# Gates, compressed scores and heads of the sparse mixer in one stage; last norm in two operations, written out in pieces

## What the kernel computes

```
proj = h @ w_in                       # 1024 columns of queries, 48 of gates
gate = sigmoid(proj[..., 1024:])      # 3 gates for each head
s = q @ k_cmp.T ; p_cmp = masked_softmax(s, cmp_end <= t)     # 15 compressed keys
p_slc = masked_softmax(q @ k_slc.T, ...)                      # causal
p_win = masked_softmax(q @ k_win.T, ...)                      # causal, window 512
out = gate0 * p_cmp @ v_cmp + gate1 * p_slc @ v_slc + gate2 * p_win @ v_win
y = out @ w_o
```

## Time and profile before

| | us |
|---|---|
| median of 3 runs | 3552.88 (3550.22 to 3556.15) |
| the profiled execution | 3553.42 |
| its span | 3551.7 |
| TensorE busy in the span | 3305.5 (93%) |
| VectorE, ScalarE, GpSimd busy | 2252.0, 1786.2, 1139.1 |
| mean granted clock of TensorE, as a share of 2.4 GHz | 0.961 |

### The profile page before, as it was taken

One profiled execution on the slowest core, in us unless ns is written; L12 is line 12 of the kernel. 1 busy time (PEld: TensorE's weight loads), 2 busy tenths in 40 slices (PEclk: granted clock), 3 DMA queues, 4 the chain that ended last, 5 costly groups with the idle time before them and its releaser, 6 DMA issues. The chain is left out here.

```text
span 3551.7 us, 64847 instructions
## 1 busy us (share of the span) xinstructions
PE 3305.5 (93%) x20998; PEld 2947.0 (83%) x20998; DVE 2252.0 (63%) x4498; ACT 1786.2 (50%) x3650; POOL 1139.1 (32%) x1179
## 2 busy tenths in 40 slices
PE   7997999999899998997999999978899889999997
PEld 7987898997599867996889999877579868899996
DVE  7966687878586553779445555554468784455555
ACT  6556545448444444557444444453345564444443
POOL 2233021226022004467633333200006676233332
PEclk9998999999999999999999999987599999999999
DMA  5540587882387443440555555633034315555554
GB/s 182 178 137 30 201 321 259 316 299 96 101 309 259 161 148 136 161 148 10 185 167 183 188 184 183 200 117 101 1 131 163 116 42 188 168 183 186 185 185 144
DMA packets 163126, 590.87 MB, mean 166 GB/s; under 512 B 18596, under 2 KB 19236, under 8 KB 162728
## 3 DMA queue, kind: packets, MB, share of 16 engines
q1 hardware_dynamic: 143824, 521.95, 44.5%
q10 hardware_dynamic: 19160, 67.18, 4.9%
HBM read 588.00 MB, written 1.06 MB: 166 GB/s over the span
## 5 line engine op out<-in xcount | busy, mean ns | idle before, releaser
L319 PEld LDWEIGHTS ps<-hT,parts 128*128 128x128 f32 x12864 | 1598.4, 194 | 82.6 <-DVE parts L143 38.1
L319 PE MATMUL ps<-hT,parts 128*128 128x256 f32 x12864 | 1615.4, 285 | 50.2 <-DVE parts L143 28.1
L143 DVE TENSOR_TENSOR parts<-ring,parts 128x512 fp32r<-128x512 f32 x1754 | 1167.3, 700 | 569.5 <-ACT parts L138 560.4
L138 ACT ACTIVATE parts<-ring 128x512 fp32r<-128x512 f32 x1930 | 1156.1, 628 | 575.7 <-PE ps L319 543.1
L319 PE MATMUL ps<-parts,gatedT 128*128 128x512 f32 x4128 | 1011.5, 397 | 7.6 <-DVE parts L143 7.6
L319 PEld LDWEIGHTS ps<-parts,gatedT 128*128 128x128 f32 x4128 | 765.3, 190 | 175.3 <-POOL gatedT L1055 7.9
L1191 POOL TENSOR_TENSOR gatedT<-acted,iota 128x256 fp32r<-128x256 f32 x264 | 167.2, 633 | 1411.6 <-PE ps L319 1196.7
L143 POOL TENSOR_TENSOR parts<-ring,parts 128x512 fp32r<-128x512 f32 x176 | 225.3, 1304 | 664.2 <-ACT parts L138 663.6
L1162 ACT ACTIVATE acted<-ps 128x256 f32<-128x256 f32 x264 | 101.9, 386 | 589.4 <-PE ps L319 589.4
L1194 POOL TENSOR_TENSOR gatedT<-acted,gatedT 128x256 fp32r<-128x256 f32 x264 | 313.4, 1187 | 20.6
L1175 DVE TENSOR_TENSOR acted<-acted,big 128x256 f32<-128x256 f32 x176 | 74.9, 425 | 362.2 <-ACT acted L1162 362.2
(11 more groups left out here) (342 smaller groups left out, 2185.1 us busy)
## 6 DMA issues: line engine op xcount, KB each, us to landing
ring<-wts SPq DMA_DIRECT2D x965, 512.0 KB, 3.5
big<-mod_wts ACTq DMA_DIRECT2D x112, 512.0 KB, 4.8
big<-rows SPq DMA_DIRECT2D x15, 512.0 KB, 5.3
big<-mod_bias ACTq DMA_DIRECT2D x14, 512.0 KB, 4.3
big<-mod_rows SPq DMA_DIRECT2D x4, 512.0 KB, 5.2
big<-peer_keys SPq DMA_DIRECT2D x2, 1024.0 KB, 5.5
x<-x_in SPq DMA_DIRECT2D x1, 1024.0 KB, 5.2
big<-s_bc ACTq DMA_DIRECT2D x4, 256.0 KB, 3.3
```

Of the source, the lines that this page charges most:

```text
L138: act.activation(self.part(n, half, 0), self.raw(n, half), ACT.Copy).then_inc(self.hi_done, 1)
L143: v.tensor_tensor(self.part(n, half, 1), self.raw(n, half), self.part(n, half, 0).bitcast(F32), ALU.subtract).then_inc(self.lo_done, 1)
L319: last = pe.matmul(out, a(x), b(y), start=start and x + y == 0, stop=stop and x == 1)
```

## The change

- `nsa` becomes one projection (now with `ahead=1`) and one stage for all the rest. In it TensorE first does the compressed scores of both query blocks, each matmul now against 128 columns (15 of them used, the rest overwritten or unread), then the gates, also 128 columns wide in place of 48, then the heads.
- The wide items come first: 32 items, wide 0 to 15, narrow 16 to 31, with no barrier between. Score banks in PSUM are four in place of two, the buffers `pr`, `prT` and `small` four in place of two, and score(i) waits for the exponentials of item i-4.
- The mask is added in place in PSUM and only to the last 128 keys of each branch (256 columns in all also for a wide item). Maximum and exponential read PSUM.
- The compressed weights are written to a padded tile `cs4`. Their copy `keep` stands on VectorE inside items 0 and 1.
- At the end of the stage ScalarE and GpSimd split the first tile of the output projection.
- `residual_ln` forms `(z - mean) * ln_g` and then `* 1/sqrt + ln_b`, one `scalar_tensor_tensor` each, all on VectorE; eps goes in as the bias of the square root, whose table is loaded up front; the output is sent as three DMAs from the same stage: 512 KB, 256 KB, 256 KB. The last stage goes.

```
-    with stage(k, "g_in b_in rooted eps_in centred gained dve") as (s, block):
+    with stage(k, "g_in b_in moments rooted finished out_done dve") as (s, block):
+        pieces = ((0, slice(0, D)), (1, slice(0, HALF)), (1, slice(HALF, D)))
+            for n, (tt, cols) in enumerate(pieces):
+                sp.wait_ge(s["finished"], n + 1)
+                sp.dma_start(rows[:, tt, cols], k.x[:, tt, cols]).then_inc(s["out_done"], 16)
...
+                st.done(v.scalar_tensor_tensor(k.tmp[:, tt, :], k.x[:, tt, :], aggr(tt)[:, 0:1], k.row[:, 0, :],
+                                               ALU.subtract, ALU.mult))
+                v.wait_ge(s["rooted"], tt + 1)
+                st.link(v.reciprocal(inverse(tt), root(tt)))
...
+                v.scalar_tensor_tensor(k.x[:, tt, cols], k.tmp[:, tt, cols], inverse(tt), k.row[:, 1, cols],
+                                       ALU.mult, ALU.add).then_inc(s["finished"], 1)
```

```
-                    [(mask, k.dram["mask"]), (cmask, k.dram["cmask"])], entry=SplitEntry(k, other_columns(k)))
+                    [(mask, k.dram["mask"]), (cmask, k.dram["cmask"])], entry=SplitEntry(k, other_columns(k)), ahead=1)
+    items = [(qt, h) for qt in (1, 0) for h in range(NH)]
...
+            def compressed(qt):
+                for h in range(NH):
+                    last = pe.matmul(k.ps[:, 4 * (1 - qt) + 2 + h % 2, 16 * h:16 * h + P], qT[rows(h), h // 2, queries(qt)],
+                                     keys_c[rows(h), NCMP * (h // NR):NCMP * (h // NR) + P], start=True, stop=True)
...
+            def score(i):
+                if i >= 4:
+                    pe.wait_ge(s["exped"], 2 * (i - 3))
...
+            compressed(1)
+            compressed(0)
             for half in range(2):
                 k.w.wait_split(pe, first, half)
...
-                        last = products(pe, k.ps[:, tt, 0:48], lambda lo: k.hT[:, lo, kc, tt * P:(tt + 1) * P],
-                                        lambda lo: k.w.part(first, half, lo)[:, q * P:q * P + 48], kc == 0, kc == KC - 1)
+                        last = products(pe, k.ps[:, tt, 0:P], lambda lo: k.hT[:, lo, kc, tt * P:(tt + 1) * P],
+                                        lambda lo: k.w.part(first, half, lo)[:, q * P:q * P + P], kc == 0, kc == KC - 1)
...
+            pe.wait_ge(s["c_maxed"], 1)
+            score(0)
+            score(1)
+            pe.wait_ge(s["c_maxed"], 2)
+            compressed_turn(0, 1)
+            compressed_turn(1, 0)
+            for i in range(n_items + 3):
+                if i + 2 < n_items:
+                    score(i + 2)
+                if 1 <= i <= n_items:
+                    turn(i - 1)
+                if i >= 3:
+                    values(i - 3)
...
+                    block_ = two(score_bank(i), qt)[:, :, nk - P:nk]
+                    v.wait_ge(s["scored"], i + 1)
+                    st.done(v.tensor_tensor(block_, block_, bc(mask[:, T - P:T].unsqueeze(1), [P, 2, P]), ALU.add))
...
+        @block.gpsimd
+        def _(pool):
+            k.w.split_lo(pool, first + 1)
```

## The result

The changed kernel takes 3513.74 us (median of four executions, 3506.64 to 3530.11), the kernel before 3554.31 beside it: ratio 0.9894, 95% interval 0.9858 to 0.9930. The forecast was 3530 in a range of 3508 to 3556. The profiled execution took 3514.44 against 3553.42: 39.0 less, where my sum had 23.3. (Medians here are over all executions of a kernel; the ratios are of means, and leave out the executions more than 1.5% above the fastest of their kernel.)

What follows compares the result with a forecast made beforehand. The prediction took TensorE at half clock in the mixer as the bound. Mixer -21.4, edge +1.8, and norm and output -3.7 sum to -23.3 from 3553.4, giving 3530 us, range 3508 to 3556.

Steps and rivals of the forecast that it cites:

- compressed scores: Mixer's first work: 64 matmuls priced from a head's narrow scores, nearly all at half clock, 18.0 us.
- gates: Mixer, after the compressed scores: 48 matmuls at half clock, 0.21 us each whatever the width, 10.1 us.
- edge to the output projection: Mixer's end: splits after the last copy delay the barrier 3.3 us, the next stage saves 1.5; net +1.8 us.
- norm and output: Kernel's end: VectorE chain done at 3543.8, last 256 KB landing 3.3 us after issue; -3.7 us.
- its own last sign: Closing test: mixer about 128 us; forecast wrong if the clock differs, all else together being worth 10 us.
- The fill: Mixer, between gates and steady heads: VectorE's path puts first transposes 8.1 us after the gates, third after 14.7.
- The same 14.9 us: Heads: full clock returns after 14.9 us of unbroken wide items, as in the kernel before, losing 7.4 us.
- The narrow items: Heads' second part: VectorE becomes the bound at 2.05 us an item against TensorE's 1.7, at full clock.
- the first rival in its second form: Mixer: clock stays up or returns within some 4 us, then the fill loses it again: 3518; whole rival's chance 0.24.
- The rival of the other side: Heads: the new order breaks the unbroken wide stretch, so the clock never lifts: +55, 3585; chance 0.08.
- That narrow items fall back to half clock: Rival, heads: VectorE's gaps put narrow items at 3.43 us in place of 2.05: +22, 3552; chance 0.13.
- In-place work in PSUM slow enough to matter: Part of a rival, heads not shortened: 0.3 us more on each VectorE step, +15, 3545; whole rival's chance 0.07.

Runs made afterwards that it cites:

- E5: The changed kernel itself, measured again unaltered: median 3507.41 us, five executions between 3497 and 3557.
- E1: The changed kernel with dummy matmuls on TensorE where it stood still while the heads fill: 3496.81 us, ratio 0.9846.
- E6: The kernel before, unmerged, with 128 columns for compressed and gate matmuls and dummy matmuls where TensorE stands still: 3531.26 us, ratio 0.9933.
- E7: The changed kernel with each block's compressed scores ordered by row half, eight heads then the other eight, not alternating: 3524.82 us, one execution.
- E10: The changed kernel with fill dummies, early output-projection split, no root table behind the query projection, and four dummies at each edge: 3490.63 us, ratio 0.9831.
- E4: The changed mixer with the last norm and output stage as in the kernel before: 3527.2 us, ratio 0.9961.
- E3: The changed kernel with the narrow items ahead of the wide ones, as before the change: 3543.68 us, ratio 0.9974.
- E2: The changed kernel with compressed matmuls put back to 15 columns and gate matmuls to 48: 3522.05 us, ratio 0.9909.

## Why the prediction was right in its range and off in its steps

| step | forecast | measured (profiled executions) |
|---|---|---|
| start of the stage | 2447.5 | 2447.3 |
| compressed scores | 18.0 | 5.4 |
| gates | 10.1 | 5.5 |
| from the gates to the third item's transposes | 14.7 | 13.7 |
| from there to the last matmul | 82.6 | 86.3 |
| mixer against before | -21.4 | -35.9 |
| edge to the output projection | +1.8 | +1.05 |
| norm and output | -3.7 | -4.9 |
| elsewhere | 0 | +0.8 |
| sum | -23.3 | -39.0 |

By its own last sign ("It is wrong if the clock differs from this") the prediction's course of the clock was wrong, and the mixer took 113.6 us where that sign had about 128. The number came into the range because the range was wide and because a part of the error was taken back: 17.2 us too much for scores and gates, 3.7 too little for the heads. That is in part luck; the same kernel measured again (E5) has its median at 3507.4, just below the range.

- **The reading of the bound was right**: TensorE at half clock was the matter, and the place. E1 shows it by adding nothing but matmuls that nobody reads, E6 by adding such matmuls and widening two kinds of matmul with the stages left as they were.
- **Compressed scores, the largest miss (12.6 us).** Two errors. I took the scores of a head as the nearest row; the compressed ones alternate between the two halves of the array's rows, which in E7 is worth 0.07 of 0.17 us each at half clock (E10 has them at 3.84 / 64 = 0.06 each at full clock, not 0.15). And I let half clock last through them, because the heads' narrow work had never lifted it. It was back 3.4 us later. The row of the old 15-column matmuls, which alternate in the same way, was in the trace (shown at E7) and would have told the price: 3.60 / 32 = 0.11 each at half clock.
- **Gates.** That 128 columns cost what 48 did was right: at half clock 0.20 us per instruction before and 9.59 / 48 = 0.20 in E6. The step failed by the clock alone, for they ran at full: 5.58 / 48 = 0.12.
- **The fill.** 1.0 us less than forecast. The terms listed up to the first head's transposes add up to 7.7, not 8.1; measured were 7.6.
- **The clock in the heads.** "The same 14.9 us" was wrong in size and in kind: 41 us in the profiled execution, 24 in E5, 58 in E4. One observation does not give a duration; what settles the time of the return is not known. From the third item's transposes to the last matmul the changed kernel takes 86.3 us, and E1, at full clock throughout, 2541.58 - 2469.63 = 71.95. So the half clock cost 14.3 us there, where I had 7.4; the same stretch at full clock was 3.2 us shorter than my 75.2. Together that is the +3.7 of the table.
- **The narrow items.** VectorE was not the bound; 1.94 us each, TensorE without gaps. My 0.3 of waits in its loop was too much. That they would hold the full clock was right.
- **The rivals.** The measured course is the first rival in its second form, a clock back within 4 us that the fill loses again; I had put it at 3518 with the family at 0.24, and the time is 3513.7. The likeliest case, one long half-clock stretch, did not come. The rival of the other side, a clock that never lifts in the heads, is not disproved: E5 had 3557 once, with a mean clock of 0.958, and E3, E2 and E4 have such executions, at 3552 to 3565, with 0.954 to 0.960 (in E3's trace the clock lifts only at the very end of the heads). Its price of 3585 was too high, mostly because it stood on scores and gates at half clock. That narrow items fall back to half clock did not come in the changed kernel, but they stay there when the fill has dropped it first (E3). In-place work in PSUM slow enough to matter did not show: the narrow items follow each other in 1.94 us.
- **The edge.** +1.05, not +1.8: the next stage starts 3.67 us after the last copy (2558.48 to 2562.15), before 1.21 (2594.63 to 2595.83). That is 2.5 us more, where I had 3.3. Of it 1.4 us come back up to the first matmul, as reckoned (1.5).
- **The norm.** The chain on VectorE took the forecast 13.7 us (3495.99 to 3509.01 + 0.66). The gain is 1.2 us more than forecast, since 256 KB landed in 2.1 us, not 3.3; I had taken the row of the same size, and it was a load into the core, not a write of the output.

## What to carry to other kernels

Where TensorE is busy without a break and yet slow, read its granted clock first, then look at what it did just before the fall: here TensorE was busy 2.34 of 4.1 us, with two pauses of 1.0 and 0.75 us, and fell to half clock; the busy share of the whole span (94%) does not show it. That cost 17 us, and twenty matmuls into an unused bank gave them back and took most of the scatter away with them. Look in the traces for the work in which the clock came back and put that first (here the alternating scores of 128 columns). Put work in which it never came back, here the narrow items, behind it. Before a duration is taken over from a similar row, compare which rows of the array follow each other, not the shape alone.

## What I had not expected of the hardware

- Heads at 1.2 GHz with TensorE busy all the time stayed there for 126 us (E3, narrow items first), or came back after 24, 41 or 58 us for the same work (E5, the changed kernel, E4).
- fp32 matmuls of 64 rows that alternate between the two row halves take 0.06 us at full clock and 0.10 at half; in a row on the same half 0.17 at half (E7). The heads' scores of the same shape take 0.30 at half clock and 0.16 at full.
- fp32r matmuls with 128 weights take 0.12 us at full clock with 128 moving columns, as they do with 256 (in the query projection before, 122 in 14.4 us, 2430.0 to 2444.4). At half clock they take 0.20 us with 48 columns (before) and with 128 (E6), and 0.22 with 128 in E7.
